# The second block's mixer stages in another order: the pairs of heads between the projections, gate sums and masks as matmuls, values by token

## The reference, cut to what matters

```python
def hybrid_mixer(h, ...):
    q_f, k_f, v_f, f_logit, q_m, k_m, v_m, c_q, c_kv, k_r = split(h @ w_in)
    F = cumsum(log_sigmoid(f_logit + b_forget))          # 4 heads of 64, causal
    o_f = dense_causal_attention(q_f, k_f, v_f, F)       # scores + F[q] - F[k]
    o_m = moba_attention(q_m, k_m, v_m, t5_table)        # 4 heads of 64, causal, T5 bias
    q_lat = rmsnorm(c_q, g_q_lat) @ w_uq                 # 8 heads of 64 + 32
    kv = rmsnorm(c_kv, g_kv_lat) @ w_ukv                 # 8 heads: key 64, value 64
    o_c = dense_causal_attention(cat(q_nope, rope(q_rot)), cat(k_nope, rope(k_r)), v_c)
    o = cat(rmsnorm(o_f, g_a), rmsnorm(o_m, g_b), rmsnorm(o_c, g_c))
    return o @ w_out

h = rmsnorm(x, g_mix_pre) * (1 + scale_a) + shift_a
x = x + gate_a * rmsnorm(hybrid_mixer(h), g_mix_post)
h = rmsnorm(x, g_ffn_pre) * (1 + scale_f) + shift_f
x = x + gate_f * rmsnorm(swiglu_2(h), g_ffn_post)
```

## Time and profile before

| what | us |
|---|---|
| median of three runs | 1864.38 (1858.51 to 1868.95) |
| the profiled execution, its own time | 1866.44 |
| its span in the profile | 1864.6 |
| mean granted TensorE clock | 0.939 |
| busy: PE, DVE, ACT, POOL | 1689.1, 1224.8, 939.7, 72.0 |
| stage b0, from the first turn of its input to that of the next stage | 1106.97 to 1283.97 |
| stage b1, the same | 1483.78 to 1660.66 |

### The profile page before, as it was taken

The page is one execution under the profiler, slowest core; times in us unless marked ns, Lnnn a source line. Parts: engine busy times, 40 slices in busy tenths (PEclk is TensorE's granted clock), DMA queues, the critical chain, the costliest instruction groups (busy, mean ns, idle before and its releaser), DMA issues.

```text
span 1864.6 us, 21975 instructions
## 1 busy us (share of the span) xinstructions
PE 1689.1 (91%) x7968; PEld 1396.9 (75%) x7968; DVE 1224.8 (66%) x1897; ACT 939.7 (50%) x1765; POOL 72.0 (4%) x131
## 2 busy tenths in 40 slices
PE   7999997899999999987999999668999896789998
...
PEclk9999997999999999997999999668999996689999
...
DMA packets 99674, 329.86 MB, mean 177 GB/s; under 512 B 18624, under 2 KB 19136, under 8 KB 99056
## 3 DMA queue, kind: packets, MB, share of 16 engines
...
## 4 chain that ended last, share of the span: by engine, by line
PE 75%; DVE 14%; ACT 7%; issue 2%; DMA 1%; POOL 0%; ACTq 0%; SPq 0%; POOLq 0%; DVEq 0%
PE PS L640 22%; PE PS L642 22%; PE PS L641 22%; DVE Wl L1382 4%; PE PS L768 2%; DVE QTl L1382 2%; ACT Wh L1031 2%; PE PS L700 1%; DVE st L1519 1%; DVE WK L1516 1%; ACT WK L1121 1%; PE PS L785 1%; ACT QTh L1031 1%; PE PS L809 1%; DVE PTl L1550 1%
## 5 line engine op out<-in xcount | busy, mean ns | idle before, releaser
L1382 DVE TENSOR_TENSOR Wl<-raw,Wh 128x1024 fp32r<-128x1024 f32 (+2 forms) x335 | 393.1, 1203 | 85.2 <-ACT Wh L1031 84.7
L640 PE MATMUL PS<-Wh,Hh 128*128 128x512 f32 (+2 forms) x1012 | 404.7, 400 | 42.7 <-DVE Hl L1432 16.8
L642 PE MATMUL PS<-Wh,Hl 128*128 128x512 f32 (+2 forms) x1012 | 398.9, 394 | 0.0
L641 PE MATMUL PS<-Wl,Hh 128*128 128x512 f32 (+2 forms) x1012 | 398.9, 394 | 0.0
L1031 ACT ACTIVATE Wh<-raw 128x1024 fp32r<-128x1024 f32 (+2 forms) x335 | 335.6, 1038 | 13.1 <-DVE GQ L1467 9.8
L640 PEld LDWEIGHTS PS<-Wh,Hh 128*128 128x128 f32 x1012 | 196.1, 194 | 87.2 <-issue 32.0
L1382 DVE TENSOR_TENSOR QTl<-raw,QTh 128x1024 fp32r<-128x1024 f32 (+1 forms) x179 | 213.3, 1214 | 21.9 <-ACT QTh L1031 21.4
L642 PEld LDWEIGHTS PS<-Wh,Hl 128*128 128x128 f32 x1012 | 196.0, 194 | 39.6
L641 PEld LDWEIGHTS PS<-Wl,Hh 128*128 128x128 f32 x1012 | 196.3, 194 | 37.0
L640 PE MATMUL PS<-QTh,Hh 128*128 128x512 f32 (+1 forms) x516 | 202.4, 392 | 4.4 <-DVE Hl L1671 3.4
L642 PE MATMUL PS<-QTh,Hl 128*128 128x512 f32 (+1 forms) x516 | 201.2, 390 | 0.0
...
## 6 DMA issues: line engine op xcount, KB each, us to landing
...
```

The source lines that it names most:

```text
L640: e.matmul(out_, xh, wh, start=start, stop=False)
L641: e.matmul(out_, xh, wl, start=False, stop=False)
L642: return e.matmul(out_, xl, wh, start=False, stop=stop)
L1382: e.tensor_tensor(low(p)[:, 0:w], raw[p % RAW][:, 0:w], high(p)[:, 0:w].bitcast(f32), ALU.subtract).then_inc(w_lo, 1)
```

## The change

It rewrites stage b and reorders some events of stage a.

- The columns of `w_in` come in another order, so that the latents and the gate are projection 0, and the queries and keys of the mixer with T5 bias (moba) projection 1; then values, then queries and keys of the forget-gate mixer (fox).
- `lat` becomes `cs`, `lt`, `lq` and `lk` (by tile), `bulk` becomes four (0: moba, 1: fox, 2 and 3: latent queries and keys). The latents are split straight out of PSUM into `QTh`/`QTl` 12 to 14.
- The pairs are moba 0 and 1, fox 2 and 3, latent 4 to 7, and their events stand between projections, latents and `wo`. Scores have one pair of banks (5 and 6) instead of two, so S waits for the pair before it: for its bias in pairs 0 and 1, else for its exponentials.
- The forget gate is no bias any more: the matmuls with the triangle accumulate into the scores' own bank (`F[q]` drops out of the softmax and is left out). The causal mask of fox and latent pairs is one matmul more for each head, identity times mask. DVE adds a bias in two pairs of eight only; ACT's exponentials read PSUM in the other six.
- The values have the turned probabilities as stationary operand and 64 columns of values as moving one: 12 or 24 matmuls instead of 6 or 12. The result lies by token in bank 3. ACT squares it with a sum (`group_squares`), POOL forms the root, DVE scales it (event R, `group_scale`), TensorE turns it (event O, 16 transposes in all), and ACT and DVE split it into `QTh`/`QTl`, from where `wo` takes it. `mix` is gone; the gain of the group norm goes into the split of the `wo` pieces.
- The slots for weights, two hooks of SP and `room` follow the new order.
- In stage a, some of S, T, V, N, `rope`, `chunks`, `wo` and the end's events change places; nothing else does.

```diff
-W_B = (512, 512, 420, 512)
+W_B = (420, 512, 512, 512)
...
-               ("S", 1, 0, 0), ("T", 0, 0, 0), ("E", 1, 0, 0), ("N", 1, 0, 0), ("proj", 3, 1, 0), ("S", 2, 0, 0),
-               ("norm", 2, 0, 0), ("V", 0, 0, 0), ("E", 2, 0, 0), ("T", 1, 0, 0), ("proj", 4, 0, 0), ("N", 2, 0, 0),
-               ("S", 3, 0, 0), ("V", 1, 0, 0), ("T", 2, 0, 0), ("E", 3, 0, 0), ("rope", 2, 0, 0), ("proj", 4, 1, 0),
+               ("S", 1, 0, 0), ("T", 0, 0, 0), ("E", 1, 0, 0), ("N", 1, 0, 0), ("S", 2, 0, 0), ("proj", 3, 1, 0),
+               ("norm", 2, 0, 0), ("V", 0, 0, 0), ("E", 2, 0, 0), ("T", 1, 0, 0), ("proj", 4, 0, 0), ("S", 3, 0, 0),
+               ("N", 2, 0, 0), ("E", 3, 0, 0), ("rope", 2, 0, 0), ("V", 1, 0, 0), ("proj", 4, 1, 0), ("T", 2, 0, 0),
                ("N", 3, 0, 0), ("V", 2, 0, 0), ("turn_qk", 2, 0, 0), ("norm", 3, 0, 0), ("S", 4, 0, 0), ("T", 3, 0, 0),
-               ("E", 4, 0, 0), ("N", 4, 0, 0), ("proj", 5, 0, 0), ("V", 3, 0, 0), ("S", 5, 0, 0), ("T", 4, 0, 0),
-               ("rope", 3, 0, 0), ("E", 5, 0, 0), ("proj", 5, 1, 0), ("V", 4, 0, 0), ("turn_qk", 3, 0, 0), ("N", 5, 0, 0),
-               ("T", 5, 0, 0), ("S", 6, 0, 0), ("V", 5, 0, 0), ("wo", (0,), 0, 0), ("chunks", 0, 0, 0), ("chunks", 1, 0, 0),
-               ("E", 6, 0, 0), ("N", 6, 0, 0), ("wo", (1,), 0, 0), ("S", 7, 0, 0), ("S", 8, 0, 0), ("T", 6, 0, 0),
-               ("E", 7, 0, 0), ("wo", (2,), 0, 0), ("wo", (3,), 0, 0), ("N", 7, 0, 0), ("S", 9, 0, 0), ("E", 8, 0, 0),
-               ("V", 6, 0, 0), ("T", 7, 0, 0), ("E", 9, 0, 0), ("N", 8, 0, 0), ("V", 7, 0, 0), ("N", 9, 0, 0),
-               ("T", 8, 0, 0), ("wo", (4,), 0, 0), ("sums", 0, 0, 0), ("T", 9, 0, 0), ("V", 8, 0, 0), ("wo", (5,), 0, 0),
-               ("rows", 0, 0, 0), ("wo", (6, 7), 0, 0), ("V", 9, 0, 0), ("sums", 1, 0, 0), *end[0], *scale[0],
-               ("wo", (0,), 1, 0), ("wo", (1,), 1, 0), ("rows", 1, 0, 0), ("wo", (2,), 1, 0), nxt[0], ("wo", (3,), 1, 0),
-               nxt[1], ("wo", (4,), 1, 0), ("wo", (5,), 1, 0), ("wo", (6, 7), 1, 0)]
+               ("E", 4, 0, 0), ("N", 4, 0, 0), ("proj", 5, 0, 0), ("V", 3, 0, 0), ("S", 5, 0, 0), ("rope", 3, 0, 0),
+               ("E", 5, 0, 0), ("proj", 5, 1, 0), ("T", 4, 0, 0), ("V", 4, 0, 0), ("turn_qk", 3, 0, 0), ("N", 5, 0, 0),
+               ("T", 5, 0, 0), ("S", 6, 0, 0), ("V", 5, 0, 0), ("chunks", 0, 0, 0), ("E", 6, 0, 0), ("N", 6, 0, 0),
+               ("wo", (0,), 0, 0), ("chunks", 1, 0, 0), ("S", 7, 0, 0), ("S", 8, 0, 0), ("T", 6, 0, 0), ("E", 7, 0, 0),
+               ("wo", (1,), 0, 0), ("wo", (2,), 0, 0), ("N", 7, 0, 0), ("S", 9, 0, 0), ("E", 8, 0, 0), ("V", 6, 0, 0),
+               ("wo", (3,), 0, 0), ("T", 7, 0, 0), ("N", 8, 0, 0), ("T", 8, 0, 0), ("E", 9, 0, 0), ("V", 7, 0, 0),
+               ("N", 9, 0, 0), ("wo", (4,), 0, 0), ("sums", 0, 0, 0), ("T", 9, 0, 0), ("V", 8, 0, 0), ("wo", (5,), 0, 0),
+               ("rows", 0, 0, 0), ("V", 9, 0, 0), ("wo", (6, 7), 0, 0), ("sums", 1, 0, 0), *end[0], ("wo", (0,), 1, 0),
+               ("wo", (1,), 1, 0), ("wo", (2,), 1, 0), ("wo", (3,), 1, 0), *scale[0], ("rows", 1, 0, 0), nxt[0], nxt[1],
+               ("wo", (4,), 1, 0), ("wo", (5,), 1, 0), ("wo", (6, 7), 1, 0)]
     else:
-        ev += [("proj", 0, 0, 0), ("proj", 1, 0, 0), *mid, ("proj", 0, 1, 0), ("proj", 1, 1, 0), ("proj", 2, 0, 0), ("proj", 2, 1, 0),
-               ("bulk", 0, 0, 0), ("proj", 3, 0, 0), ("proj", 3, 1, 0), ("lat", 0, 0, 0),
-               *(x for p in range(PAIRS["b"] + 1) for x in (
-                   ([("S", p, 0, 0)] if p < PAIRS["b"] else []) + ([("T", p - 1, 0, 0)] if p else [])
-                   + ([("E", p, 0, 0)] if p < PAIRS["b"] else []) + ([("V", p - 1, 0, 0)] if p else [])
-                   + ([("N", p, 0, 0)] if p < PAIRS["b"] else []))), ("mix", 0, 0, 0),
-               *(("wo", (c,), 0, 0) for c in range(8)), *end[0], *scale[0], *(("wo", (c,), 1, 0) for c in range(8)), *nxt]
+        ev += [("proj", 0, 0, 0), ("proj", 1, 0, 0), *mid, ("proj", 0, 1, 0), ("fg", 0, 0, 0), ("cs", 0, 0, 0),
+               ("proj", 1, 1, 0), ("cs", 1, 0, 0), ("fg", 1, 0, 0), ("bulk", 0, 0, 0), ("fg", 2, 0, 0), ("proj", 2, 0, 0),
+               ("lt", 0, 0, 0), ("proj", 2, 1, 0), ("S", 0, 0, 0), ("E", 0, 0, 0), ("proj", 3, 0, 0), ("N", 0, 0, 0),
+               ("proj", 3, 1, 0), ("T", 0, 0, 0), ("S", 1, 0, 0), ("E", 1, 0, 0), ("V", 0, 0, 0), ("R", 0, 0, 0),
+               ("N", 1, 0, 0), ("lq", 0, 0, 0), ("T", 1, 0, 0), ("lk", 0, 0, 0), ("bulk", 1, 0, 0), ("V", 1, 0, 0),
+               ("R", 1, 0, 0), ("lq", 1, 0, 0), ("S", 2, 0, 0), ("E", 2, 0, 0), ("lk", 1, 0, 0), ("N", 2, 0, 0),
+               ("O", 0, 0, 0), ("S", 3, 0, 0), ("T", 2, 0, 0), ("bulk", 2, 0, 0), ("E", 3, 0, 0), ("V", 2, 0, 0),
+               ("R", 2, 0, 0), ("N", 3, 0, 0), ("O", 1, 0, 0), ("bulk", 3, 0, 0), ("T", 3, 0, 0), ("S", 4, 0, 0),
+               ("E", 4, 0, 0), ("V", 3, 0, 0), ("N", 4, 0, 0), ("R", 3, 0, 0), ("S", 5, 0, 0), ("T", 4, 0, 0),
+               ("V", 4, 0, 0), ("E", 5, 0, 0), ("O", 2, 0, 0), ("N", 5, 0, 0), ("wo", (0,), 0, 0), ("S", 6, 0, 0),
+               ("T", 5, 0, 0), ("E", 6, 0, 0), ("wo", (1,), 0, 0), ("O", 3, 0, 0), ("wo", (2,), 0, 0), ("V", 5, 0, 0),
+               ("N", 6, 0, 0), ("R", 4, 0, 0), ("S", 7, 0, 0), ("T", 6, 0, 0), ("E", 7, 0, 0), ("O", 4, 0, 0),
+               ("V", 6, 0, 0), ("wo", (3,), 0, 0), ("wo", (4,), 0, 0), ("N", 7, 0, 0), ("wo", (5,), 0, 0), ("T", 7, 0, 0),
+               ("V", 7, 0, 0), ("wo", (6,), 0, 0), ("wo", (7,), 0, 0), ("R", 5, 0, 0), ("O", 5, 0, 0), ("wo", (0,), 1, 0),
+               ("wo", (1,), 1, 0), ("gp", 0, 0, 0), ("wo", (2,), 1, 0), *end[0], ("wo", (3,), 1, 0), *scale[0],
+               ("wo", (4,), 1, 0), ("wo", (5,), 1, 0), nxt[0], nxt[1], ("wo", (6, 7), 1, 0)]
...
                 for i, item in enumerate(it["heads"]):
+                    at = [PS[:, score_bank(stage, p, k), i * nk:i * nk + nk] for k in range(2)]
+                    if it["group"] == "x":
+
+                        for k in range(2):
+                            for c in range(nk // 128):
+                                for part in range(2):
+                                    o = 4 * c + 2 * i + k
+                                    e.matmul(at[k], lfr[:, part, o:o + 1].to_broadcast([128, 128]), Ur[:, c, 0:nk],
+                                             start=c == 0 and part == 0, stop=False)
+                            e.matmul(at[k][:, nk - 128:nk], IM[:, 0, :], IM[:, 1, :], start=False, stop=False)
                     for j in range(3):
                         for k, ((qh, ql), (kh, kl)) in enumerate(item):
-                            ins = e.matmul(PS[:, score_bank(p, k), i * nk:i * nk + nk], ql if j == 2 else qh,
-                                           kl if j == 1 else kh, start=j == 0, stop=j == 2)
+                            ins = e.matmul(at[k], ql if j == 2 else qh, kl if j == 1 else kh,
+                                           start=j == 0 and it["group"] != "x", stop=j == 2)
+                        if j == 0 and it["group"] == "l":
+                            for k in range(2):
+                                e.matmul(at[k][:, nk - 128:nk], IM[:, 0, :], IM[:, 1, :], start=False, stop=False)
...
+            def values_b(stage, p):
+                it, gp = pairs_of[stage][p], pair0[stage] + p
+                l = stage[1]
+                if p in (1, 2, 3, 4, 6):
+                    e.wait_ge(o_copy, 6 * l + (p if p < 6 else 5))
+                if p == 0:
+                    e.wait_ge(j_dve, dve_steps(stage, 2, 1))
+                elif p == 4:
+                    e.wait_ge(c_dve, 4 * l + 4)
+                for i, unit in enumerate(it["v"]):
+                    e.wait_ge(t_lo, entry[stage, "T", p, i] + 1)
+                    for k in range(2):
+                        o = it["chunk"] + 128 * i + 64 * k
+                        for c, (vh, vl) in enumerate(unit):
+                            m = slice((2 * c + k) * 128, (2 * c + k) * 128 + 128)
+                            ins = three(PS[:, 3, o:o + 64], PTh[:, i, m], PTl[:, i, m], vh[:, half[k]], vl[:, half[k]], c == 0,
+                                        c == len(unit) - 1)
+                ins.then_inc(s_v, 1)
+            def turn_group(stage, x):
+                l, key = stage[1], (stage, "O", x, 0)
+                n, src, _, _ = group_of(x)
+                e.wait_ge(o_copy, 6 * l + x + 1)
+                if before_in[key] is not None:
+                    e.wait_ge(t_lo, before_in[key] + 1)
+                for c in range(n // 128):
+                    ins = e.transpose(PS[:, bank_of[key], c * 128:c * 128 + 128], src[:, c * 128:c * 128 + 128], ident)
+                ins.then_inc(o_turn, 1)
...
-            def group_norms(stage):
-                l = stage[1]
-                e.wait_ge(t_lo, entry[stage, "T", PAIRS["b"] - 1, 1] + 1)
-                for t in range(2):
-                    for ch in range(8):
```

(53 more changed lines are left out.)

674 lines of the change are left out of this document (349 added, 325 removed).

## The result

The changed kernel takes 1839.9 us (median of four, 1839.3 to 1843.2) against 1864.8, a ratio of 0.987 (95% interval 0.984 to 0.990). I had forecast 1800, range 1772 to 1838. The sign was right and the size was not: 25 us of 64. The profiled execution took 1839.27 us, its span is 1837.4, 27.2 less than before.

The account below looks back on a forecast made before the run. PE sets the time; the engine-to-engine chain bounds stage b after its projections. 1866.4 less 60 (both stages b) less 5 (both stages a) is 1801.4 for the profiled execution, 1799.4 at the median, say 1800; range 1772 to 1838.

Parts of the forecast that it names:

- PE's work: In stage b: 51 us of projections, 63.9 of mixed stretch, 10.9 of `wo` of tile 1; PE is not relieved.
- M: Mixed stretch of stage b between projections and `wo` of tile 1: 63.9 us of PE work.
- The head: Start of stage b: projections, the input's turns and their waits, less 8 transposes that move later, 51 us.
- The walk's waits: Walking M's written order with prices: some 13 us of PE waits, thus 77 us for M, yardstick 0.83.
- How full PE will be: In M: yardstick 0.75, between stage a's 0.69 and the walk's 0.83, giving a stage b of 147.1 us.
- Half clock (1): Rival: remaining waits keep PE at 1.2 GHz through much of M; yardstick 0.62, stage b 165, kernel 1838 us; chance 0.19.
- the yardstick: Product of PE's busy share and granted clock, how much of a full PE is at work; 0.75 forecast for M.
- `wo` of tile 1 stays a stream of 10.9: At the end of stage b: 48 matmuls at 0.227 us run as a stream, 10.9 us.
- Stage a: Reordered stage a: 2.5 us better per stage, 5 for both, bounds 5 worse to 5 better per stage.
- Value matmuls: In M: 144 matmuls of 64 columns, 14.4 to 17.3 us at full clock, 17.3 taken; 31.7 at half clock.
- The gate sums and masks: Added to the scores' banks in M: 48 matmuls at 0.12 us, 5.8 us; nothing taken for tiling mode changes.
- FFN's start: PE's wait for weights there stays about 2.5 us, at most four pieces (5 us) worse.

Follow-up runs that it names:

- e2: Changed kernel with divisions of pairs 1 and 3 ahead of the previous pair's values, bulk 3 before group 2's norm, in stage b: 1840.6 us, ratio 0.988.
- f10: e1 plus a second order for pairs 1 and 3 of stage b, without weight splits at V 0 and V 2: 1827.3 us, ratio 0.982.
- e8: e1 plus idle PE matmuls before T(1) and before the last transposes of bulk 3 in stage b: 1822.1 us, ratio 0.978.
- f9: e8 plus stage b's value matmuls made 128 columns wide instead of 64, result unchanged: 1808.5 us, ratio 0.973.
- f12: e1 plus value matmuls 128 columns wide instead of 64, without idle work: 1822.7 us, ratio 0.980.
- e1: Changed kernel with tile 0's chain (squares to scaled x) put ahead of the weight splits at the end of stage b: 1828.4 us, ratio 0.981.
- e4: Changed kernel with the stages a back in the order of the kernel before, stages b as changed: 1846.0 us, ratio 0.990.
- e5: Changed kernel leaving out one of three products of every value in stage b, 96 matmuls a stage instead of 144: 1827.2 us, ratio 0.979.
- e6: Changed kernel without the 48 matmuls a stage that add gate sums and masks to stage b's scores: 1843.0 us, ratio 0.989.

## Why the prediction was right or wrong

**PE's work: right.** M was 63.9 us, of which 1.6 (turning latents, S(0)) lie ahead of T(0): 62.3, against 64.7 measured. The head, 51, and this 1.6 measured 51.3. One comparison beside the sum was wrong: 63.9 is not "about what the rest had before", since the 62.9 of before hold `wo` of tile 1 and the 63.9 do not. Like for like it is 74.8 against 62.9: the change gives PE 12 us more work a stage.

**The walk's waits: right in size, half right in place.** I counted 13 us; 15.5 came. T(1) waits 5.7 where I had 4. The 3 us that I put before T(3) are 3.9 in bulk 3 ahead of it. Moving them did not help (e2, f10).

**How full PE will be: this step failed.** I took 0.75 from stage a and kept the walk's 0.83 as the upper bound; M gave 81.92 / 97.40 x 0.79 = 0.66, under my lower bound of 0.69. The waits are not the difference: half the clock is, 17.2 us in M where 0.75 leaves 62.3 / 0.75 - 62.3 - 13 = 8. Of the 14.3 us that M takes beyond 62.3 / 0.75, some 9 are half clock, 2.5 waits and 2.4 work. I had written that the clock is at half where PE waits again and again and full in streams, so that the clock would follow the waits. e8 shows it falling where PE has been busy for 3 us, behind a wait of only 0.5, and f9 shows it staying full there once the value matmuls are wider; f12, with the wider matmuls and the long wait, falls again. Both terms count, and the forecast had only one. Half clock (1), which I gave 0.19 (the prediction's sentence on the clock gate calls it the second rival, it is the first), has its number within 2 us (1838) and its stage of 165, but that is in part luck: the yardstick is 0.66 and not 0.62, and the rest stands at the end of the stage.

**`wo` of tile 1 stays a stream of 10.9: failed.** It took 16.4 to the next turn, with two of its eight chunks (2.7) only behind it, so 19.1 for the same work. My sum put the chain from tile 0's squares to the scaled x at nothing and gave no reason. PE waited nowhere in this stretch before; now the chain's place among the weight splits had moved, and PE waited 7.2 us for it. e1 puts it at 11.5 us for two stages.

With both repaired b0 is 145.9 and b1 146.6, against a forecast of 147.1. This is close in part by luck: the two chunks of `wo` are not in it (2.7), useless matmuls are (32 x 0.227 = 7.3), and the stage behind b0 is 204.8, 5.4 longer than in the changed kernel. The yardstick for M fits better: (75.86 x 0.96 - 7.3) / 85.70 = 0.77, where I had 0.75.

**The smaller steps.** Stage a: 5 forecast, 5 to 6 by e4. Value matmuls: 17.3 forecast at 0.12; they are 0.11 apart, and e5 puts a removed one at 0.13 to 0.16, half clock included. The gate sums and masks: 5.8 us of PE's time forecast, nothing on balance by e6. The Trainium skill's page "TensorEngine Tiling (Array Packing)", section "Key Properties", has the rule that I weighed, that a change of the tiling mode drains TensorE. No cost of it is seen in e6, though the lower clock there could hide a small one. FFN's start: 2.5 to 5 forecast; the stage behind b0 was 0.4 us shorter and the last FFN 4.0 longer, with 2.7 us of `wo` moved into each. The last FFN also has a clock of 0.83 from 1649.5 to 1669.5; that part I did not test.

The Trainium skill's page "TensorE: Matmul & The Clock Gate", section "HAM oscillation — how this bites in real kernels", gives two cures for a throttled PE, fewer waits between matmuls and padding thin ones. Here reordering brought 2 us fewer waits at best (f10) and no time; idle work in them and padding from 64 to 128 columns each worked a little (7.5 and 6.6 us by the medians), and both together more.
